# Exponents of the scan from running sums, turned modulation rows on VectorE, and an earlier entry of the gated attention

## The reference, cut to what matters

```
modulation:  silu(c) @ mod_w[i] + mod_b[i]      (12 row pieces of 512 per layer; here both c_ctx and c)

ssd_scan (16 heads of 64, 2 groups, forward and backward):
  seg    = ac[:, :, :, None] - ac[:, :, None]          # ac = cumsum(da)
  decay  = exp(where(tril, seg, -inf))
  scores = einsum('bclgn,bcsgn->bclsg', cc, bc) * decay
  y_diag = einsum('bclsge,bcsgep->bclgep', scores, xc)
  states, y_off: products with the group's B and C, scaled by exp(ac), carried from chunk to chunk

gla_scan (4 heads, keys 128, values 256, forward and backward):
  rel = exp(gcum_t - gcum_s) per key channel; att = sum_d q * rel * k; o = att @ v + (q exp(gcum)) @ S
  then  o = rms_norm(o) * silu(r)
```

## Time and profile before

| | us |
|---|---|
| median of 3 runs | 1884.34 (1884.04 to 1887.13) |
| profiled execution | 1884.42 |
| its span, first to last instruction | 1882.6 |
| TensorE busy in the span | 1802.7 (96%) |
| VectorE / ScalarE / GpSimd busy | 1151.3 / 640.3 / 127.2 |
| SSD loop with its opening, 203.42 to 327.12 | 123.70, TensorE busy 123.32 |
| entry of the gated attention, 450.36 to 459.14 | 8.78, TensorE busy 5.28 |

### The profile page before, as it was taken

How to read it: one execution, slowest core, us unless ns; L and a number is a source line. 1 busy time by engine, 2 the same in 40 slices (tenths; PEclk the granted TensorE clock), 3 DMA queues, 4 the chain that set the end, 5 groups by cost and what they waited for, 6 DMA issues and landing times. The chain is left out here.

```text
span 1882.6 us, 35011 instructions
## 1 busy us (share of the span) xinstructions
PE 1802.7 (96%) x14348; PEld 1436.7 (76%) x14348; DVE 1151.3 (61%) x2295; ACT 640.3 (34%) x1474; POOL 127.2 (7%) x122
## 2 busy tenths in 40 slices
PE   6999999998998999999999999999989998999997
PEld 2447777887667868888888878887766666989997
DVE  2653676534787553445544377776859868766765
ACT  4121223633552031111100043675256876132210
POOL 0000232000000100000001000001211111000000
PEclk9999999999999999999999999999989999999999
DMA  7433201123402322222233132222222011534443
GB/s 304 179 117 137 90 23 45 56 102 143 151 4 90 146 68 90 89 78 82 88 140 134 67 109 87 74 68 91 91 92 91 2 40 65 203 132 170 157 168 101
DMA packets 28174, 195.99 MB, mean 104 GB/s; under 512 B 3020, under 2 KB 4301, under 8 KB 5870
## 3 DMA queue, kind: packets, MB, share of 16 engines
q1 hardware_dynamic: 27970, 193.61, 28.8%
q10 hardware_dynamic: 44, 0.14, 0.0%
HBM read 192.69 MB, written 1.05 MB: 103 GB/s over the span
## 5 line engine op out<-in xcount | busy, mean ns | idle before, releaser
L2015 ACT ACTIVATE ws_sb<-psum 128x256 f32<-128x256 f32 (+4 forms) x446 | 187.1, 421 | 851.6 <-PE psum L946 820.5
L946 PE MATMUL psum<-arena_sb,ws_sb 128*128 128x256 f32 (+3 forms) x2208 | 377.9, 323 | 2.4 <-DVE hT_sb L2664 0.9
L946 PEld LDWEIGHTS psum<-arena_sb,ws_sb 128*128 128x128 f32 (+1 forms) x2208 | 317.0, 183 | 42.3 <-issue 13.8
L946 PE MATMUL psum<-hT_sb,ring_sb 128*128 128x256 f32 (+3 forms) x1344 | 326.9, 390 | 2.4 <-ACT hT_sb L2015 1.8
L946 PEld LDWEIGHTS psum<-hT_sb,ring_sb 128*128 128x128 f32 (+1 forms) x1344 | 228.3, 189 | 80.9 <-issue 57.4
L2664 DVE TENSOR_TENSOR ws_sb<-ws_sb,psum 128x256 f32<-128x256 f32 (+2 forms) x310 | 121.2, 400 | 186.7 <-PE psum L946 86.1
L946 PE MATMUL psum<-arena_sb,ring_sb 128*128 128x256 f32 (+1 forms) x1168 | 214.2, 333 | 3.1 <-ACT arena_sb L2015 1.7
L946 PEld LDWEIGHTS psum<-arena_sb,ring_sb 128*128 128x128 f32 x1168 | 183.7, 191 | 22.4 <-DVE ws_sb L2664 2.7
L2664 DVE TENSOR_TENSOR ws_sb<-ring_sb 128x512 f32<-128x512 f32 (+1 forms) x166 | 116.4, 701 | 103.3 <-PE psum L946 72.6
L946 PE MATMUL psum<-ring_sb,hT_sb 128*128 128x256 f32 (+4 forms) x1024 | 168.4, 347 | 0.8 <-ACT hT_sb L2015 0.8
L946 PEld LDWEIGHTS psum<-ring_sb,hT_sb 128*128 128x128 f32 (+1 forms) x1024 | 135.9, 174 | 37.6 <-issue 17.2
(11 more groups left out here) (226 smaller groups left out, 2262.9 us busy)
## 6 DMA issues: line engine op xcount, KB each, us to landing
ring_sb<-w SPq DMA_DIRECT2D x142, 1024.0 KB, 4.9
arena_sb<-w SPq DMA_DIRECT2D x12, 1024.0 KB, 15.1
hT_sb<-w SPq DMA_DIRECT2D x12, 1024.0 KB, 4.9
ring_sb<-w SPq DMA_DIRECT2D x8, 768.0 KB, 4.4
xT_sb<-x SPq DMA_DIRECT2D x2, 2048.0 KB, 10.0
const_sb<-w SPq DMA_DIRECT2D x3, 1024.0 KB, 6.7
const_sb<-consts SPq DMA_DIRECT2D x1, 2048.0 KB, 10.1
extra_sb<-w SPq DMA_DIRECT2D x1, 1024.0 KB, 7.0
```

What stands on the lines that cost most here:

```text
L946: return nc.tensor.matmul(o, l, r, start=start, stop=stop, **kw)
L2015: return nc.scalar.activation(o, i, func, **kw)
```

## The change

1. **Exponents.** With da and -da as 32 rows per direction, TensorE makes running sums once (`running_sums`, in unit 2 of stage qk0) and ScalarE writes two operands of 64 partitions. GpSimd masks one of them per step (`head_sums`, one operation on 64 partitions in place of two on 128). `decay(w)` is now two products of K=32 on rows 64 to 95 and 96 to 127, one a direction, into bank 4 (forward) and bank 5 (backward). As neither is masked, ScalarE copies the backward one to SBUF (`backward_copied`), VectorE takes the smaller of the two (`least`), and ScalarE's Exp then reads SBUF. On TensorE `decay(w + 1)` moves behind the gate products, and waits for `least(w)`, since both banks are used by every step.
2. **Scores.** VectorE's 4 multiply-adds become ScalarE's 4 scaled copies (`g_dt_fwd`, so 8 in all) and one 128x512 add.
3. **Turned rows.** VectorE turns the row bank in 32x32 blocks from PSUM (`late_turned`, `pause_turned`), TensorE adds the four parts with one product of 32 columns (`added_parts`), and VectorE adds the bias in 4 operations of 32 partitions (`with_bias`). ScalarE's copies go, also those inside the norms.
4. **Entry of the gated attention.** `near_levels(0, 0)` runs behind unit 2 of r0, `near_levels(0, 1)` inside unit 3, with their Exp operations inside ScalarE's part of unit 3 and `weigh(0)` inside VectorE's; `mod1_rows(0)` moves between the levels of pair 1. The Silu of the last r0 unit is left to one operation at p = 13, with two table loads.

The diff, cut to its core:

```diff
@@ TensorE
+            def running_sums():
+
+                pe.wait_ge(S["ssd_signed"], 1)
+                for j in range(TT):
+                    for d in DIRS:
+                        last = mm(psum[64 + 32 * d:96 + 32 * d, 6, j * P:(j + 1) * P], da_signed[:, j, d].rearrange("p a b -> p (a b)"), upto_incl[d])
+                last.then_inc(S["dt_turned"], 1)
...
                 def decay(w):
-                    if w > 1:
-                        pe.wait_ge(S["ssd_exp"], w - 1)
+
+                    if w > 0:
+                        pe.wait_ge(S["ssd_least"], w)
+                    pe.wait_ge(S["ssd_r"], w + 1)
+                    j = w // 4
                     for d in DIRS:
-                        u = 2 * w + d
-                        pe.wait_ge(S["ssd_r"], u + 1)
-                        mm(psum[:, 4 + w % 2, :], beyond[d], g_decay[:, d].rearrange("p a b -> p (a b)"),
-                           start=(d == 0), stop=(d == 1)).then_inc(S["ssd_seg"], 1)
+                        rows_ = slice(64 + 32 * d, 96 + 32 * d)
+                        last = mm(psum[:, 4 + d, :], wide[rows_, 2, j * P:(j + 1) * P], head_sums[rows_, w % 2].rearrange("p a b -> p (a b)"))
+                    last.then_inc(S["ssd_seg"], 1)
 
                 decay(0)
                 for w in range(16):
-                    if w + 1 < 16:
-                        decay(w + 1)
                     for n in (2 * w + 2, 2 * w + 3):
                         if n < 32:
                             z0_part(n)
                         else:
                             first_values(n - 32)
+                    if w + 1 < 16:
+                        decay(w + 1)
...
+            def added_parts(bank, turned_rows):
+
+                return mm(psum[:, bank, 0:32].rearrange("p (b r) -> p b r", r=2), cm("pick"),
+                          turned_rows.rearrange("p (b r) -> p b r", r=32)[:, :, 0:2])
...
-                for p in range(2):
-                    for hh in range(2):
-                        near_levels(p, hh)
-                    tile_levels(p)
+                tile_levels(0)
+                pe.wait_ge(S["k_tok"], GLA_H)
+                near_levels(1, 0)
+                mod1_rows(0)
+                near_levels(1, 1)
+                tile_levels(1)
+                units_taken("r0")
+                pe.wait_ge(S["gla_zeroed"], 1)
@@ ScalarE
+                def backward_copied(w):
+
+                    act.wait_ge(S["ssd_seg"], w + 1)
+                    if w > 1:
+                        act.wait_ge(S["ssd_p"], w - 1)
+                    own(f(e_seg[:, w % 2].rearrange("p a b -> p (a b)"), psum[:, 5, :], ACT.Copy).then_inc(S["ssd_copied"], 1), S["ssd_copied"])
+
+                backward_copied(0)
                 for w in range(16):
...
-                        ins = f(g_dt[:, w % 2, i], g_mask[:, 1, g, j], ACT.Copy, scale=dt[:, j, 16 + h:17 + h])
+                        f(g_dt[:, w % 2, i], g_mask[:, 1, g, j], ACT.Copy, scale=dt[:, j, 16 + h:17 + h])
+                        ins = f(g_dt_fwd[:, w % 2, i], g_mask[:, 0, g, j], ACT.Copy, scale=dt[:, j, h:h + 1])
                     own(ins.then_inc(S["ssd_dt"], 1), S["ssd_dt"])
-                    act.wait_ge(S["ssd_seg"], 2 * w + 2)
-                    own(f(e_seg[:, w % 2], psum[:, 4 + w % 2, :].rearrange("p (a b) -> p a b", a=4), ACT.Exp).then_inc(S["ssd_exp"], 1), S["ssd_exp"])
+                    act.wait_ge(S["ssd_least"], w + 1)
+                    own(f(e_seg[:, w % 2], e_seg[:, w % 2], ACT.Exp).then_inc(S["ssd_exp"], 1), S["ssd_exp"])
+                    if w + 1 < 16:
+                        backward_copied(w + 1)
...
+                    if p == 13:
+                        load_tables(SILU)
+                        gated(3, "up_near", r0[:, :, 3 * CB:4 * CB])
+                        load_tables(LOG_EXP)
@@ VectorE
+            def with_bias(layer, at, bank):
+
+                parts = psum[:, bank, 0:32].rearrange("p (t u r) -> p t u r", u=4, r=2)
+                bias = cl("mod_b", 48 * layer + at, 4)
+                for u in range(4):
+                    rows_ = slice(32 * u, 32 * u + 32)
+                    ins = tt(mod[rows_, layer, at:at + 4], parts[rows_, :, u], bc(bias[rows_], 2, 2), ALU.add)
+                return ins
+
+            def late_turned(q):
+
+                dve.wait_ge(S["late_rows"], q + 1)
+                if q > 0:
+                    dve.wait_ge(S["late_columns"], q)
+                own(V.transpose(late_row, psum[:, 4, :]).then_inc(S["late_turned"], 1), S["late_turned"])
...
+                def least(w):
+
+                    dve.wait_ge(S["ssd_copied"], w + 1)
+                    e = e_seg[:, w % 2].rearrange("p a b -> p (a b)")
+                    own(tt(e, e, psum[:, 4, :], ALU.min).then_inc(S["ssd_least"], 1), S["ssd_least"])
+
                 def scores(w):
 
-                    j, g, h0 = w // 4, w // 2 % 2, w % 4 * 4
                     dve.wait_ge(S["ssd_dt"], w + 1)
-                    for i in range(4):
-                        ins = stt(g_dt[:, w % 2, i], g_mask[:, 0, g, j], dt[:, j, h0 + i:h0 + i + 1], g_dt[:, w % 2, i], ALU.mult, ALU.add)
-                    link(ins)
+                    link(tt(g_dt[:, w % 2], g_dt[:, w % 2], g_dt_fwd[:, w % 2], ALU.add))
...
+                least(0)
                 inputs(0)
                 for w in range(16):
                     scores(w)
+                    if w + 1 < 16:
+                        least(w + 1)
                     if w > 0:
                         accumulate(w - 1)
@@ GpSimd
-            for u in range(32):
-                w, d = u // 2, u % 2
-                at = d * 16 + w % 4 * 4
-                if u > 1:
-                    pool.wait_ge(S["ssd_seg"], u - 1)
-                own(tt(g_decay[:, d], bc(da[:, w // 4, at:at + 4], 2, P), bc(upto_incl[d], 1, 4)).then_inc(S["ssd_r"], 1), S["ssd_r"])
+            pool.wait_ge(S["ssd_sums"], 1)
+            for w in range(16):
+                j, at = w // 4, w % 4 * 4
+                if w > 1:
+                    pool.wait_ge(S["ssd_seg"], w - 1)
+                own(tt(head_sums[sum_rows, w % 2], bc(moving_sums[:, j * P:(j + 1) * P], 1, 4),
+                       bc(cl("sum_heads", at, 4)[sum_rows], 2, P)).then_inc(S["ssd_r"], 1), S["ssd_r"])
```

More of the change, by code:

```diff
@@ L987, in between @@
                     turn_dt()
+                if stage == "qk0" and g == 2:
+                    running_sums()
                 for half in LATE_AT.get((stage, g), ()):
@@ L1168, in pause_columns @@
                 layer, first, banks = PAUSES[tag]
-                copied, columns = (S["mod_copied"], S["mod_columns"]) if layer else (S["late_copied"], S["late_columns"])
+                turned, columns = (S["mod_copied"], S["mod_columns"]) if layer else (S["late_turned"], S["late_columns"])
                 for k in range(2):
-                    pe.wait_ge(copied, first + k + 1 - (0 if layer else MOD_FIRST))
-                    for t in range(4):
-                        last = nc.tensor.transpose(psum[:, banks[k], t * P:(t + 1) * P], wide[:, k, t * P:(t + 1) * P], ident)
-                    last.then_inc(columns, 1)
+                    pe.wait_ge(turned, first + k + 1 - (0 if layer else MOD_FIRST))
+                    added_parts(banks[k], wide[:, k, :]).then_inc(columns, 1)
+            def added_parts(bank, turned_rows):
+                return mm(psum[:, bank, 0:32].rearrange("p (b r) -> p b r", r=2), cm("pick"),
+                          turned_rows.rearrange("p (b r) -> p b r", r=32)[:, :, 0:2])
             def keep_clock(n):
@@ new lines, in near_levels @@
+            def near_levels(p, hh):
+                d, k, h, j = pair_at(p)
+                c = cms(f"lvl{d}", 8)
+                at = (h + hh) * P
+                u = LEVEL_UNITS * p + 2 * hh
+                if u >= 2:
+                    pe.wait_ge(S["gla_exp"], u - 1)
+                for i in range(2):
+                    toks = halves(i)
+                    last = mm(psum[:, level_bank(u + i), 0:64 * LEV].rearrange("p (a b) -> p a b", b=64),
+                              gk[toks, j, d, at:at + P], c[toks, 0:LEV, toks])
+                last.then_inc(S["gla_lv"], 1)
@@ new lines, in tile_levels @@
+            def tile_levels(p):
+                d, k, h, j = pair_at(p)
+                c = cms(f"lvl{d}", 8)
+                u = LEVEL_UNITS * p + 4
+                pe.wait_ge(S["gla_exp"], u - 2)
+                if k < 3:
+                    last = mm(psum[:, level_bank(u), 0:2 * P], beyond[d], gk[:, j, d, h * P:(h + 2) * P])
+                for hh in range(2 if k > 0 else 0):
+                    last = mm(psum[:, level_bank(u), (2 + hh) * P:(3 + hh) * P], gk[:, j, d, (h + hh) * P:(h + hh + 1) * P], c[:, LEV, :])
+                last.then_inc(S["gla_lv"], 1)
@@ L2391, in unit_copied @@
                 near, far, up_far, up_near = unit_dests(stage, j)
[L2392 removed]
+                gated_now = stage == "r0" and j + 1 < SEVENS[stage][1]
```

(11 more changed lines are left out.)

194 lines of the change are left out of this document (94 added, 100 removed).

## The result

The changed kernel takes 1947.72 us (median of 4 runs, 1940.48 to 1949.24) against 1885.74 before (one execution more than in the table ahead): ratio 1.0315, 95% interval 1.0291 to 1.0339. It is slower, as forecast, and the wait that was forecast is there, but it is slower by 62 us instead of 36, and outside the range (1903 to 1940). The profiled execution has a span of 1945.9 us against 1882.6, 63.3 more.

What follows compares the result with a forecast made beforehand. TensorE, busy for 96% of the span, was taken as the bound. SSD loop +30.6, clock +10, turned rows -1.5 and gated attention's entry -3.3 sum to +35.8 on 1884.4: 1920 us, range 1903 to 1940 (8 in 10).

Steps and rivals of the forecast that it cites:

- the clock's term: SSD loop: slow work at the lower clock after eight long TensorE waits, 1.25 us each, +10 us, bounds 0 and 13.6.
- the clock stays low: Rival, SSD loop: slow spells run into each other, costing about 40 us instead of 10; 1950 us, chance 0.08.
- The queue's wait: SSD loop, steps 1 to 14: TensorE's state pair waits for `accumulate`, queued on VectorE behind the waiting `least`; +38.2 us.
- The cheaper pair: SSD loop, exponents: two K=32 products side by side save 0.45 us a step, 16 times; -7.2 us.
- The own waits: SSD loop: the idle time TensorE already had there before the change goes; -0.4 us.
- Scores by scaled copies: SSD loop: ScalarE's added copies and VectorE's changed work never come last; priced at nothing.
- Turned rows and running sums: Outside the loop: cheaper row turning, less time for running sums and VectorE's longer list; -1.5 us, bounds -4 and +2.
- The entry: Entry of the gated attention: first scores come sooner after r0, less a late Silu; -3.3 us, bounds -5 and +1.
- That Silu: Gated attention, p = 13: two table loads and a Silu make ScalarE's last far and near copies late by about 0.5 us.
- the pair is not side by side: Rival, SSD loop: the two shallow exponent products run one after the other, 0.86 us more a step; 1934 us, chance 0.10.
- the clock holds: Rival, SSD loop: waits as worked out, but work between them keeps the clock up; 1910 us, chance 0.22.
- the covered case: Rival, SSD loop: `least` is released during the gate products, so the state pair does not wait; 1872 us, chance 0.03.

Runs made afterwards that it cites:

- the repaired kernel: The changed kernel with two calls exchanged in VectorE's list, `accumulate(w - 1)` now ahead of `least(w + 1)`: 1873.92 us, ratio 0.9946 to the kernel before.

## Why the prediction was wrong

The step that failed is the clock's term, "I take 1.25 of 1.7, 8 times: +10 us". The changed kernel's loop is 66.0 us longer than that of the repaired list, which has the same instructions. By the table above 38.0 of it are the waits; the other 28.0 are work at half speed, nearly three times the term and twice its upper bound of 13.6. Two things were off. Each of the eight long waits cost 2.5 to 2.7 us, 21.0 in all: the spells are 6.8 us long (read in stretches of 0.1 us), of which 1.4 to 1.9 fall into the wait, where the single one behind the earlier trace rows from which the price was taken is 3.4. And of the six short waits, which it left out, four cost 1.74 us each, 7.0 in all. Why the spells were twice as long is open: the same single wait of 2.64 us costs 0, 1.6 or 2.9 us in the ten traces, so the price came from one draw of something that varies, and no run shows whether standing in a row makes it dear.

That the time comes out at the 1950 of the rival "the clock stays low" is luck. Its condition, that the spells run into each other, is not met, since the clock comes back in every step, and its 40 us are not the 28 of the loop. The rest of the way is the lost gain at the gated attention (2.8 us) and the 5.6 us behind it, which no term had; without these two the time would lie at the upper end of the range. The page of the Trainium skill that the prediction cites ("TensorE: Matmul & The Clock Gate", section "HAM oscillation — how this bites in real kernels") tells of a loop that pays on every pass. This trace agrees: all eight long waits are followed by slow work. The prediction took the rule and had too small a price for each pass.

The other terms, as they came out:

- The queue's wait, +38.2 forecast: 38.0 by distances, with 3.48 to 3.57 us for 3.55, 2.11 for 2.11 and 1.39 for 1.39, eight, two and four times. (The profile's idle times, 36.0, are shorter, because the records' ends overhang by 0.16 us.)
- The cheaper pair, -7.2: in the repaired kernel a step is 7.32 us for the 7.78 of the earlier trace rows, 0.46 less, against 0.45. The 0.2 us for each change of the row split holds, and so does side by side.
- The own waits, -0.4: gone, as forecast. The repaired loop is 7.6 shorter than before in all.
- Scores by scaled copies, priced at nothing: right, ScalarE is busy for 68.53 us of the loop's 117.89 and VectorE for 78.06, and nobody waits for them.
- Turned rows and running sums, -1.5: the rows alone gain 2.4 in the head (146.59 to 144.22), and the running sums cost 1.6 to 2.3 of it again rather than 1.2 (the head is 145.81 to 146.54 in the seven kernels that have them). From the first product behind the gated attention to the end the repaired kernel is 0.3 shorter than before, with spells of equal length. In all the -1.5 came out as -0.3 to -1.0.
- The entry, -3.3: from r0's last product to the first scores are 4.89 us (5.2 forecast). From the first product on 33 rows to the first one behind the gated attention are 240.69 us before, 237.44 in the repaired kernel, 3.3 less as forecast, and 240.17 in the changed one. There 2.7 go to longer spells behind the same idle times: 48 products behind 2.64 us take 8.54 us for the repaired kernel's 7.23, and the work behind the Silu's idle time 6.11 for 4.68. That Silu, forecast at about 0.5, holds TensorE up by 2.65 us, of which 0.6 were idle before, and 0.9 of it are to be had back by distances.

One reading in the rivals is off without touching the rest: by the prediction's own terms `accumulate` ends 2.3 to 4.5 us after `decay`'s issue, not 1.63 to 4.5, since its shortest form takes 0.69. The rival that the pair is not side by side fell by the 1.06 us from pair to diagonal; that the clock holds, by the 0.81 of the loop's row; the covered case by VectorE's rows. The repaired kernel, 1873.9, comes out where the covered case was put, 1872: the change is good but for the place of one call.

## What to carry to other kernels

An operation that waits belongs behind everything in its queue that is already free to run and that the bounding engine needs sooner; moving what it waits for (here `decay`) and what stands behind it (here `accumulate`) are the same decision, to be read from both lists together. Where TensorE stands for 1.4 to 3.6 us in every step, book the wait and then much of it again for slow work behind it: here 28 us on top of 38. The price of one wait taken from one trace is one draw; look for the same wait in several traces before multiplying it. And a product that nobody reads is a cheap probe: it tells in one run what the wait costs and what the clock.

## What the runs showed of the hardware that was not expected

- The price of a wait of TensorE varies for one and the same wait: alone ahead of the same 48 products, 2.64 us cost 0, 1.6 or 2.9 us of slow work in ten traces. In one trace two waits of 3.5 us, each behind filled ones, cost 1.47 and 2.40, and the two that followed 2.56 each.
- A wait of 1.4 us can bring the lower clock on: in the changed kernel's loop the second of two costs 1.74 us, the first nothing. A single one of 1.57 us cost nothing in one kernel and 1.6 us in another, and of two executions with 1.97 and 1.95 us ahead of the same products one kept 1.00 and one had 0.51.
- Filling 2.6 of 3.4 idle us with products on all 128 rows kept the clock at 1.00 through the whole loop, with 0.77 us still idle.
- Products on 32 of 128 rows in each of sixteen steps left the granted clock at 1.00 as long as TensorE did not stand.
